# Nine inverse square roots of a two-block transformer step, made by ScalarE's square root, VectorE's reciprocal and one Newton step

## The reference

```python
def rmsnorm(x, g):
    xf = x.astype(jnp.float32)
    y = xf * lax.rsqrt(jnp.mean(xf * xf, axis=-1, keepdims=True) + EPS) * g.astype(jnp.float32)
    return y.astype(x.dtype)
...
x = x + 0.5 * swiglu(rmsnorm(x, ffn1_norm), ffn1_wgu, ffn1_wdown)
q = rmsnorm(zq.reshape(B, S, N_Q_HEADS, HEAD_DIM), q_norm)
c = jax.nn.silu(layernorm(u, conv_ln_g, conv_ln_b)) @ conv_proj
...
h = rmsnorm_2(x, g_pre[0]) * (1 + sc1) + sh1
x = x + 0.5 * gt1 * rmsnorm_2(swiglu_2(h, w_gu1, w_dn1), g_post[0])
...
o_a = rmsnorm_2(gla_chunked(q, k, v, log_a), g_gla) * jax.nn.silu(r_a)
```

## Time and profile before

| what | value |
|---|---|
| median of 3 runs | 1496.27 us (1492.18 to 1497.22) |
| profiled execution, its time | 1489.66 us |
| span of the profile | 1487.9 us |
| PE busy | 1371.2 us (92%) in 6461 matmuls |
| DVE busy | 980.0 us (66%) in 1420 instructions |
| ACT busy | 751.2 us (50%) in 1146 instructions |
| POOL busy | 144.7 us (10%) |
| mean granted TensorE clock | 0.963 of full speed |
| chain that ended last | PE 80%, DVE 10%, ACT 4%, DMA 2%, issue 2% |

### The profile page before, as it was taken

One profiled execution on the slowest core, in us unless ns is written; L12 is line 12 of the kernel. 1 busy time (PEld: TensorE's weight loads), 2 busy tenths in 40 slices (PEclk: granted clock), 3 DMA queues, 4 the chain that ended last, 5 costly groups with the idle time before them and its releaser, 6 DMA issues.

```text
span 1487.9 us, 16986 instructions
## 1 busy us (share of the span) xinstructions
PE 1371.2 (92%) x6461; PEld 1138.8 (77%) x6461; DVE 980.0 (66%) x1420; ACT 751.2 (50%) x1146; POOL 144.7 (10%) x164
## 2 busy tenths in 40 slices
PE   6999999679978999999799999699999999699997
PEld 4888778557757788877688878588887887588885
DVE  5767755898876677766767774658775555655543
ACT  5445446748764544445544443456444563454431
POOL 3000003833420010000000100000000000000000
PEclk9999999879988999999899999799999999799999
DMA  9887755523334588875378776355553354366662
GB/s 281 277 268 265 260 167 162 177 71 100 98 102 127 170 267 280 269 255 177 118 246 262 257 251 176 110 170 162 150 156 86 100 160 151 100 185 187 188 190 71
DMA packets 166338, 269.58 MB, mean 181 GB/s; under 512 B 14001, under 2 KB 114521, under 8 KB 166257
## 3 DMA queue, kind: packets, MB, share of 16 engines
q1 hardware_dynamic: 153952, 226.66, 49.8%
q0 software_dynamic: 12000, 41.48, 8.2%
q10 hardware_dynamic: 304, 0.35, 0.1%
HBM read 267.40 MB, written 1.05 MB: 180 GB/s over the span
## 4 chain that ended last, share of the span: by engine, by line
PE 80%; DVE 10%; ACT 4%; DMA 2%; issue 2%; POOL 1%; SPq 0%; DVEq 0%; ACTq 0%; POOLq 0%
PE ps L1445 26%; PE ps L1433 15%; PE ps L1435 15%; PE ps L1434 14%; DVE w_lo L836 2%; POOL y L454 1%; PE ps L1530 1%; ACT w_hi L473 1%; DMA raw<-in_ffn_wgu_dram 1%; PE ps L1766 1%; PE ps L1464 1%; DMA raw<-in_ffn_wdown_dram 1%; PE ps L1566 1%; PE ps L1549 1%; PE ps L1603 1%
## 5 line engine op out<-in xcount | busy, mean ns | idle before, releaser
L836 DVE TENSOR_TENSOR w_lo<-raw,w_hi 128x1024 fp32r<-128x1024 f32 (+1 forms) x431 | 521.6, 1222 | 335.9 <-ACT w_hi L473 334.8
L473 ACT ACTIVATE w_hi<-raw 128x1024 fp32r<-128x1024 f32 (+1 forms) x431 | 450.9, 1054 | 397.9 <-DMA raw<-in_ffn_wgu_dram 112.2
L1433 PE MATMUL ps<-w_hi,a_hi 128*128 128x512 f32 (+1 forms) x1152 | 464.4, 403 | 6.8 <-DVE a_lo L901 5.4
L1435 PE MATMUL ps<-w_hi,a_lo 128*128 128x512 f32 (+1 forms) x1152 | 450.9, 391 | 0.0
L1434 PE MATMUL ps<-w_lo,a_hi 128*128 128x512 f32 (+1 forms) x1152 | 450.3, 391 | 0.0
L1433 PEld LDWEIGHTS ps<-w_hi,a_hi 128*128 128x128 f32 x1152 | 220.9, 192 | 50.1 <-DVE a_lo L901 6.3
L1435 PEld LDWEIGHTS ps<-w_hi,a_lo 128*128 128x128 f32 x1152 | 220.0, 191 | 46.3
L1434 PEld LDWEIGHTS ps<-w_lo,a_hi 128*128 128x128 f32 x1152 | 221.0, 192 | 41.3
L454 POOL TENSOR_TENSOR y<-y,prod 128x512 f32<-128x512 f32 x60 | 91.6, 1526 | 160.6 <-ACT prod L591 155.7
L1445 PE MATMUL ps<-w_hi,hid_hi 128*128 128x512 f32 x336 | 104.0, 391 | 0.0
L1445 PE MATMUL ps<-w_lo,hid_hi 128*128 128x512 f32 x336 | 103.5, 389 | 0.0
(11 more groups left out here) (315 smaller groups left out, 1268.2 us busy)
## 6 DMA issues: line engine op xcount, KB each, us to landing
raw<-in_ffn_wgu_dram SPq DMA_DIRECT2D x176, 256.0 KB, 4.0
raw<-in_w_in_dram SPq DMA_DIRECT2D x88, 512.0 KB, 3.7
raw<-in_w_gu_dram SPq DMA_DIRECT2D x176, 256.0 KB, 3.2
ada<-in_w_ada_dram POOLq DMA_DIRECT2D x72, 512.0 KB, 5.4
raw<-in_ffn_wdown_dram SPq DMA_DIRECT2D x44, 512.0 KB, 4.2
raw<-in_w_dn_dram SPq DMA_DIRECT2D x44, 512.0 KB, 3.6
raw<-in_w_in_dram SPq DMA_DIRECT2D x36, 256.0 KB, 3.1
raw<-in_w_out_dram SPq DMA_DIRECT2D x16, 512.0 KB, 3.6
```

The costliest lines, as they stand in the source:

```text
L473: act.activation(w_hi[:, u % RING, 0:nk * n], raw[:, u % RING, 0:nk * n], ACT.Copy).then_inc(hi_ready, 1)
L836: dve.tensor_tensor(w_lo[:, u % RING, 0:nk * n], raw[:, u % RING, 0:nk * n], w_hi[:, u % RING, 0:nk * n].bitcast(F32), ALU.subtract).then_ ...
L1433: pe.matmul(dst(t)[:, 0:n], a[0], slot(u, w_hi, kk, n), start=kc == 0, stop=False)
L1435: i = pe.matmul(dst(t)[:, 0:n], a[1], slot(u, w_hi, kk, n), start=False, stop=kc == KC - 1)
```

## The change

Nine of the 14 roots (`ROOTS`: the heads, the layer norm, the three norms "f2", "mix2", "f3", the norms behind the three products of block two, and the linear attention) are made by `inverse_root`. VectorE still forms v = scale * src + EPS. Beside it ScalarE takes the square root of the same sum, with the scale and a tile `epsb` that holds EPS as bias, except for the layer norm, where it roots VectorE's v (signalled by `var_ready`). VectorE waits for `sqrt_ready`, takes the reciprocal, and makes one Newton step: 5 instructions in place of 11. The roots of "f0", "mix", "f1", "gate" and the embedding stay as they were.

`load_table(f)` is an activation of one element for each partition, whose only use is that the compiler puts the table load ahead of it. There are 12 of them; the program's table loads go from 19 to 28, since three of the 12 (those of Silu) stand for loads that the first gate activation behind them caused before.

```diff
+            def load_table(f):
+                if tables[0] >= 1:
+                    act.wait_ge(sem("table_used"), tables[0])
+                tables[0] += 1
+                act.activation(epsb[:, 1:2], epsb[:, 0:1], f).then_inc(sem("table_used"), 1)
+            def square_root(key, dst, src, scale):
+                act.activation(dst, src, ACT.Sqrt, scale=scale, bias=epsb[:, 0:1]).then_inc(sem("sqrt_ready"), 1)
+            def norm_root(key):
+                act.wait_ge(sem("ss_ready"), 2 * NORM[key] + 2)
+                square_root(key, rt[:, 1, 0:2], ss[:, :], 1.0 / D)
+            def post_root(key):
+                act.wait_ge(sem("pss_ready"), 2 * POST[key] + 2)
+                square_root(key + "_post", rt[:, 1, 0:2], pss[:, :], 1.0 / D)
...
                 hidden_hi(f, UPB - 1)
+                if f >= 2:
+                    load_table(ACT.Sqrt)
                 w.to(dn + 7)
...
                 w.to(M1 + slot + 4)
+                if slot == Q1:
+                    load_table(ACT.Sqrt)
...
                     products(3, TAP2 if slot < 27 else 2 * TAP2)
+                if slot == Q1:
+                    act.wait_ge(sem("heads_summed"), 1)
+                    square_root("heads", rt[:, 1, :], rt[:, 2, :], 1.0 / HD)
+                    load_table(ACT.Sigmoid)
...
                     act.activation(v, v, ACT.Sigmoid).then_inc(sem("gates_ready"), 1)
+            load_table(ACT.Sqrt)
             w.to(u_ap + KC + 3)
...
             w.to(u_cp + 2)
+            act.wait_ge(sem("var_ready"), 1)
+            act.activation(lnt[:, 1, :], lnt[:, 0, :], ACT.Sqrt).then_inc(sem("sqrt_ready"), 1)
+            load_table(ACT.Silu)
...
+            load_table(ACT.Sqrt)
             w.to(u_pg + KC + 4)
             norm_squares("f2", h)
+            norm_root("f2")
             turned_hi("f2")
+            load_table(ACT.Silu)
             ffn_part(2)
             post_squares("f2", h, ffn[2][1] + FC)
+            post_root("f2")
             w.to(ffn[2][1] + FC + 4)
             norm_squares("mix2", h)
+            norm_root("mix2")
             turned_hi("mix2")
...
+            load_table(ACT.Sqrt)
             for t in range(T):
                 act.wait_ge(sem("gla_out"), t + 1)
...
+            act.wait_ge(sem("gla_squares"), T * GH)
+            square_root("gla", ga_ss[:, 3, :], ga_ss[:, 0, :], 1.0 / GDV)
+            load_table(ACT.Exp)
...
+            load_table(ACT.Sqrt)
             w.to(u_wo2 + 4)
...
+            post_root("mix2")
             w.to(u_wo2 + KC + 4)
             norm_squares("f3", h)
+            norm_root("f3")
             turned_hi("f3")
+            load_table(ACT.Silu)
             ffn_part(3)
             post_squares("f3", h, ffn[3][1] + FC)
+            post_root("f3")
...
+            def inverse_root(key, dst, src, scale, tmp, signal=None, count=0):
+                v, a = tmp[0], tmp[1]
+                i = dve.tensor_scalar(v, src, scale, EPS, ALU.mult, ALU.add)
+                if key == "ln":
+                    i.then_inc(sem("var_ready"), 1)
+                    dve.wait_ge(sem("var_ready"), 1)
+                else:
+                    then(i)
+                dve.wait_ge(sem("sqrt_ready"), ROOTS.index(key) + 1)
+                then(dve.reciprocal(dst, a))
+                then(dve.tensor_tensor(a, dst, dst, ALU.mult))
+                then(dve.scalar_tensor_tensor(a, a, -0.5, v, ALU.mult, ALU.mult))
+                i = dve.scalar_tensor_tensor(dst, a, 1.5, dst, ALU.add, ALU.mult)
...
-                rsqrt(rstd[:, :], ss[:, :], 1.0 / D, small(rt), sem("rstd_ready"), q + 1)
+                if key in MODS:
+                    inverse_root(key, rstd[:, :], ss[:, :], 1.0 / D, small(rt), sem("rstd_ready"), q + 1)
+                else:
+                    rsqrt(rstd[:, :], ss[:, :], 1.0 / D, small(rt), sem("rstd_ready"), q + 1)
```

More of the change, by code:

```diff
@@ L141, in two_blocks @@
         nsink = keep("nsink", [P, NH])
+        epsb = keep("epsb", [P, 2])
         kd, KD0, _ = place("kd", [P, GH * S])
@@ L248, in two_blocks @@
         NMIX = 4 * len(MIX)
+        Q1 = 4 * MIX_AT[("qkv", 2)] + 4
         def cols_units(W, c0, n, c1=None):
@@ L341, in two_blocks @@
         FFN = ["f0", "f1", "f2", "f3"]
+        ROOTS = ["heads", "ln", "f2", "f2_post", "mix2", "gla", "mix2_post", "f3", "f3_post"]
         XQ = 4
@@ L475, in _ @@
             w = Stream(hi_part)
+            tables = [0]
+            def load_table(f):
[11 more added lines that the diff above has]
+                square_root(key + "_post", rt[:, 1, 0:2], pss[:, :], 1.0 / D)
             def norm_squares(key, junk):
@@ L631, in _ @@
             folded_norm("mix")
+            act.wait_ge(sem("eps_ready"), 1)
             for slot in range(NMIX):
@@ L861, in rsqrt @@
                         then(i)
+            def inverse_root(key, dst, src, scale, tmp, signal=None, count=0):
[11 more added lines that the diff above has]
+                i = dve.scalar_tensor_tensor(dst, a, 1.5, dst, ALU.add, ALU.mult)
+                if signal is not None:
+                    i.then_inc(signal, 1)
+                    dve.wait_ge(signal, count)
+                else:
+                    then(i)
             def small(r, n=2):
@@ L1008, in add_post @@
                 dve.wait_ge(sem("pss_ready"), 2 * n + 2)
-                rsqrt(prs[:, :], pss[:, :], 1.0 / D, small(rt))
+                inverse_root(key + "_post", prs[:, :], pss[:, :], 1.0 / D, small(rt))
                 dve.wait_ge(sem("post_made"), 2 * n - 1)
@@ L1108, in _ @@
             row_scales("f0")
+            dve.memset(epsb[:, 0:1], EPS).then_inc(sem("eps_ready"), 1)
             dve.wait_ge(sem("const_landed"), 16)
@@ L1125, in _ @@
             z = qkv[:, :, 0:18 * HD].rearrange("p t (h d) -> p t h d", d=HD)
-            Q1 = 4 * MIX_AT[("qkv", 2)] + 4
             def shape_heads(part):
@@ L1131, in shape_heads @@
                     then(dve.tensor_tensor(qsq[:, :, :, :], z, z, ALU.mult))
-                    then(dve.tensor_reduce(rt[:, 2, :].rearrange("p (t h) -> p t h", t=T), qsq[:, :, :, :], AX, ALU.add))
+                    dve.tensor_reduce(rt[:, 2, :].rearrange("p (t h) -> p t h", t=T), qsq[:, :, :, :], AX, ALU.add)\
+                       .then_inc(sem("heads_summed"), 1)
+                    dve.wait_ge(sem("heads_summed"), 1)
                 elif part == 1:
-                    rsqrt(rs36[:, :], rt[:, 2, :], 1.0 / HD, small(rt, 36))
+                    inverse_root("heads", rs36[:, :], rt[:, 2, :], 1.0 / HD, small(rt, 36))
                 elif part in (2, 3):
@@ L1207, in _ @@
             dve.wait_ge(sem("y_summed"), 2)
-            rsqrt(lnb[:, 1, :], ps[:, 5, 0:S], 1.0 / D, [lnt[:, 0, :], lnt[:, 1, :]])
+            inverse_root("ln", lnb[:, 1, :], ps[:, 5, 0:S], 1.0 / D, [lnt[:, 0, :], lnt[:, 1, :]])
             def scaled(c):
@@ L1372, in _ @@
             dve.wait_ge(sem("gla_squares"), T * GH)
-            rsqrt(ga_ss[:, 1, :], ga_ss[:, 0, :], 1.0 / GDV, [ga_ss[:, 2, :], ga_ss[:, 3, :]])
+            inverse_root("gla", ga_ss[:, 1, :], ga_ss[:, 0, :], 1.0 / GDV, [ga_ss[:, 2, :], ga_ss[:, 3, :]])
             for t in range(T):
```

## The result

| | before | changed |
|---|---|---|
| median | 1493.38 us (16 runs, 1488.72 to 1498.63) | 1482.65 us (16 runs, 1477.79 to 1493.62) |
| ratio | 1 | 0.9938, 95% interval 0.9918 to 0.9958 |
| profiled execution / its span | 1489.66 / 1487.9 us | 1490.57 / 1488.8 us |
| PE busy | 1371.2 us | 1376.6 us |
| mean granted clock, profiled | 0.963 | 0.963 |

A forecast was written before the change was run, and what follows sets the result against it. The prediction took PE's waits on the latency of small root instructions as the bound; 6.2 + 1.04 + 0.9 - 0.8 = 7.4 us saved from 1496.27 gave 1488.9 us, range 1482.5 to 1494.

The forecast's parts named there:

- the rival of the clock: Behind "mix2" and "f3" the clock returns sooner, and the heads lose nothing: 13.5 us saved, 1482.8 us; chance 0.20.
- three signs of being wrong: ScalarE's root starting behind v, PE waiting for `w_lo` anywhere, or the wait for `cub` growing by several us.
- Six small roots: Two-value roots of "f2", "mix2", "f3" and three post norms: 1.04 us saved each, 6.2 in all.
- The linear attention's root: Root of 8 values in the linear attention: saves 1.04 us, with PE's wait behind it at 2.3.
- The layer norm's root: Root of 256 values per partition: 4.03 us instead of 4.92, 0.9 saved (bounds 2.1 saved, 0.8 lost).
- The heads' root: Root of 36 values, ScalarE waiting in slot 20: 0.8 us lost, between 1.3 saved and 1.8 lost.
- The table loads: Nine added loads, each holding ScalarE 1.5 us with its tiny activation, all hidden behind other waits: cost 0.
- The rule of a drain behind each load: Rival of long loads: each table switch holds ScalarE 1.3 us beyond its row, 3.7 us lost, 1492.6 us; chance 0.08.
- Sum: All terms over the whole kernel: 6.2 + 1.04 + 0.9 - 0.8 = 7.4 us saved.
- ScalarE as the bound of the first mixer: Slots 21 to 23 take 7.0 us each, `cub` 8 us late, 15 lost against 8.2 saved, 1503.1 us; chance 0.04.
- the slow crossing: ScalarE's root starts later than v, so each root saves 0.6 us, not 1.04: 1492.0 us; chance 0.12.

The follow-up runs named there:

- later heads: The changed kernel with ScalarE's root of the heads and the Sigmoid load one slot later, behind slot 21's unit and products; ratio 0.9902.
- the loads alone: The kernel before with only the twelve `load_table` calls added, all nine roots made the old way on VectorE; ratio 1.0001.
- doubling the loads: The changed kernel with another table loaded first in each of the twelve places, meant to hold ScalarE 3.0 us instead of 1.5; ratio 0.9978.
- two Newton steps: The kernel before with two Newton steps instead of three in the nine roots, on VectorE alone, with no table loads; ratio 0.993.
- Six Newton steps: The kernel before with six Newton steps instead of three in the nine roots, nothing else changed; ratio 1.0126.

## Why the prediction was right, and where not

The time, 1482.65 us, lies just inside the lower edge of the range (1482.5), 6 us under the forecast of 1488.9. That it lies inside is partly luck, and so is that it meets the 1482.8 of the rival of the clock: that number was added up from heads that win 1.3 us, and they lose 1.7. As a ratio the two are nearer: 1488.9 / 1496.27 is 0.9951, inside the interval of 0.9918 to 0.9958. The median of the kernel before had been 1496.27 in the three runs shown and was 1493.38 over sixteen. So 2.9 of the 6.2 us are the kernel before, measured anew. The mechanism forecast is the one seen, and none of the three signs of being wrong came: ScalarE's root starts with v, PE waits for no `w_lo`, and the wait for `cub` did not grow by several us.

- **Six small roots.** 6.2 forecast, 0.98 each or 5.9 seen. The reciprocal started 0.39 behind v, not 0.34. The two sources of the crossing, the tile operand (0.29 long where 0.203 plus 0.1 was put) and the semaphore, came out right to 0.06 (the crossing took 0.10, not 0.04).
- **The linear attention's root.** 1.04 forecast, 1.0 seen in the wait (2.3 to 1.3).
- **The layer norm's root.** 0.9 forecast, 0.8 seen. The reciprocal took 1.75 us where the two small forms of the earlier trace rows had given 1.68. With the prediction's estimate of 2.3 us from the repeat count in the Trainium skill, "VectorE: DVE Perf Modes", "First, the fixed hardware budget", the root would not have won 0.8 but 0.2; the trace decides against that estimate. (The terms of the forecast add up to 4.04, not 4.03.)
- **The heads' root.** 0.8 lost forecast, 1.7 lost seen. This is the term that was mis-sized. VectorE's wait ahead of `w_lo` was right (2.92, forecast 2.94), and the root of five instructions still took 4.1 us from 293.61 to its end, where the working had 1.3 plus a third of the extra. The hold-ups did not shrink with the number of instructions, but fell on those that came at POOL's moments. The later heads show that this is a matter of the moment: the same five took 1.3 us. The longer root is 0.7 of the 0.9 us missed. Two things that the working left out nearly cancel in the rest: the steps between the root and `cub` took 1.3 us longer (10.46 against 9.15), and the squares ahead of the sums 1.1 less.
- **The table loads.** 0 forecast, 0 seen, by the loads alone (1.0001). ACT_TABLE_LOAD appears 28 times at 1.28, as forecast. The rule of a drain behind each load (the Trainium skill, "ScalarE: Activation LUTs", "What ACT_TABLE_LOAD costs") has nothing to show here: the tiny activation starts 0.01 us behind the load in all twelve places, and doubling the loads lengthens the waits by at most the loads themselves (1.5 at `cub`).
- **Sum.** 7.4 forecast, 6.1 in the waits and at the end, 9.3 in time.
- **ScalarE as the bound of the first mixer** and **the slow crossing** did not happen: `cub` came 1.7 later, not 8, and each root saved 0.98, not 0.6.
- **The clock.** In the profile of the changed kernel this rival's mechanism isn't there: behind the shorter stretches of "mix2" and "f3" the clock is at 0.50 as before, and at "f2", which had been the model for the good case, it is at 0.50 too. But behind "f3" the loss comes in two sizes. It is 4.1 to 4.5 us of work in the three unfilled profiles with an idle stretch of 11.5 us or more, and in four of the six with a shorter one (8.4 to 10.4), the changed kernel among them; in the other two, the later heads and two Newton steps, it is 1.6 and 1.7. There the clock is back within 4 us of the first product. The later heads, whose products start at 1273.2:

```profile
1272.00:1276.00 4.00, 2.82 (x13) 0.50 0.00 0
1276.00:1280.00 4.00, 3.45 (x16) 0.92 0.00 0
```

  So a shorter stretch can give what the rival said, but does not always; two of six against none of three can't show it, and among the six the shortest stretch (8.4) lost 4.3 and the longest (10.4) 1.7. What decides stays open. In size, too, something like the rival is there. Over all runs the changed kernel's mean granted clock is 0.9659 against 0.9613, and within one and the same kernel a run with 0.001 more clock is 1.2 us shorter on average. By that rate the difference would be 5.5 us, of which a part is low clock in stretches that have only become shorter and cost nothing; the three us that the time has beyond the waits fit into it. Six Newton steps show no such extra; two Newton steps do (10.5 against 6.1), and the later heads (14.7 against 8.4). Where in the program the better clock lies, one profile of each kernel can't tell, since runs of one kernel differ by as much. That the 3 us are clock is argued from these means, not shown; within the interval of the ratio they may also be next to none (6.3 against 6.1).

## What to carry to other kernels

Where an engine waits at the end of a chain of tiny instructions, count the instructions: at a few values for each partition each costs about 0.2 us whatever it computes, so a shorter formula on the same engine can give as much as a move to another one. Before adding a step that makes a busy engine wait in the middle of a stream, move the wait to where its answer is already there; here one slot later turned a loss of 1.7 us into a gain of 0.6. And when a gain is a fraction of a per cent, read it in the waits, and take PE's busy time for the same matmuls as the measure of what the clock did to this one execution.

## What the runs showed of the hardware

- The same 6461 matmuls took PE 1371.2, 1376.6 and 1364.1 us of busy time (before, changed, later heads), and with the loss to the clock taken off 1342.4 in all three; the other six profiles without fillers give 1340.5 to 1343.1. Runs of the changed kernel with a clock of 0.961 took 1489.4 and 1493.6 us, those with 0.970 and 0.971 took 1477.8 and 1480.9: the spread goes with the clock.
- TensorE's clock can be kept up through a wait by matmuls that nobody reads (1.00 instead of 0.50 behind "f3", transposes 1.97 instead of 3.68 us). The Trainium skill, "TensorE: Matmul & The Clock Gate", Part 1, says that the array falls to 1.2 GHz when idle and comes back to 2.4 GHz when busy, which agrees with "f3". At "mix2" the clock fell although the stretch had been filled, behind a gap and matmuls of 32 columns, and stayed down under full work, which that rule alone does not explain.
- A reciprocal costs by the value: 0.158 us for 2, 0.170 for 4, 0.38 for 36, 1.75 for 256, some 6.3 ns for each further value, where other operations on 256 values took 0.42.
- VectorE instructions, small ones too, are held up by up to 1.1 us each at moments when POOL is at its additions, and not at all when POOL waits. In the profile of before, 12 of the 231 that overlap work of POOL took over 0.15 us longer than the shortest of their line and form, and none of the 1116 beside an idle POOL.
